# Two-layer decoder, expert layer: hidden columns in four chunks of 896, ScalarE's hand-overs one split earlier

## The reference

```python
def swiglu(h, wg, wu, wd):
    return (jax.nn.silu(h @ wg) * (h @ wu)) @ wd

def moe_swiglu(h, w_router, w_gate, w_up, w_down):
    logits = (h @ w_router).astype(jnp.float32)
    top_v, top_i = lax.top_k(logits, TOP_K)                 # TOP_K = 2
    top_w = jax.nn.softmax(top_v, axis=-1)
    gates = ...                                             # (tokens, 8), two nonzero a row
    for e in range(N_EXPERTS):                              # 8 experts, EXPERT_FF = 3584
        y = y + gates[..., e:e + 1] * swiglu(h, w_gate[e], w_up[e], w_down[e])
    return y
```

## Time and profile before

| | |
|---|---|
| median of 3 runs | 1429.4 us (1425.54 to 1433.12) |
| profiled execution | 1420.63 us, its span 1418.8 us |
| granted TensorE clock, mean | 0.986 |
| PE busy | 1369.0 us, 96% of the span |
| DVE busy | 1097.6 us, 77% |
| ACT busy | 940.6 us, 66% |
| DMA | 439.13 MB in 136643 packets, mean 310 GB/s |
| chain that ended last | PE 73%, DVE 17%, ACT 5%, DMA 3%, issue 3% |

### The profile page before, as it was taken

The page is one execution under the profiler, slowest core; times in us unless marked ns, Lnnn a source line. Parts: engine busy times, 40 slices in busy tenths (PEclk is TensorE's granted clock), DMA queues, the critical chain, the costliest instruction groups (busy, mean ns, idle before and its releaser), DMA issues.

```text
span 1418.8 us, 16608 instructions
## 1 busy us (share of the span) xinstructions
PE 1369.0 (96%) x6550; PEld 1143.2 (81%) x6550; DVE 1097.6 (77%) x871; ACT 940.6 (66%) x767; POOL 49.3 (3%) x51
## 2 busy tenths in 40 slices
PE   8999999999999999999999999999999999999887
PEld 7886788887988788877888878878887878888766
DVE  4786644556465988888898898798898889888796
ACT  3565534335455677777777788687777777777764
POOL 0000000000010000000000000000000000002000
PEclk9999999999999999999999999999999999999998
DMA  9744455555632899999999999999999989999993
GB/s 311 214 159 149 155 205 178 178 179 177 224 119 92 334 373 382 379 387 399 322 407 390 364 400 407 393 366 398 379 374 414 408 324 397 394 368 392 412 360 115
DMA packets 136643, 439.13 MB, mean 310 GB/s; under 512 B 11520, under 2 KB 28912, under 8 KB 120816
## 3 DMA queue, kind: packets, MB, share of 16 engines
q1 hardware_dynamic: 130688, 424.24, 80.0%
q0 software_dynamic: 3392, 12.07, 2.5%
q10 hardware_dynamic: 2480, 1.69, 0.4%
HBM read 432.20 MB, written 5.78 MB: 309 GB/s over the span
## 4 chain that ended last, share of the span: by engine, by line
PE 73%; DVE 17%; ACT 5%; DMA 3%; issue 3%; ACTq 0%; SPq 0%; DVEq 0%
PE ps L2003 18%; PE ps L2005 18%; PE ps L2004 18%; DVE lo L1286 12%; PE ps L2575 7%; PE ps L2495 4%; PE ps L2496 4%; ACT hi L790 2%; DMA raw<-in_od_w_gate_dram 2%; PE ps L2560 1%; DMA wr<-in_od_w_router_dram 1%; ACT work L1098 1%; DVE work L1312 0%; PE ps L2299 0%; DMA x<-in_x_dram 0%
## 5 line engine op out<-in xcount | busy, mean ns | idle before, releaser
L1286 DVE TENSOR_TENSOR lo<-raw,hi 128x2048 fp32r<-128x2048 f32 (+1 forms) x403 | 904.9, 2285 | 102.9 <-ACT hi L790 101.2
L790 ACT ACTIVATE hi<-raw 128x2048 fp32r<-128x2048 f32 (+1 forms) x403 | 766.8, 1914 | 206.4 <-PE ps L2005 157.0
L2003 PE MATMUL ps<-hi,xT_hi 128*128 128x512 f32 (+1 forms) x752 | 294.6, 392 | 7.2 <-DVE lo L1286 4.6
L2005 PE MATMUL ps<-hi,xT_lo 128*128 128x512 f32 (+1 forms) x752 | 290.0, 386 | 0.0
L2004 PE MATMUL ps<-lo,xT_hi 128*128 128x512 f32 (+1 forms) x752 | 289.7, 385 | 0.0
L2495 PE MATMUL ps<-hi,xT_hi 128*128 128x512 f32 x448 | 187.4, 418 | 12.0 <-DVE lo L1286 11.0
L2496 PE MATMUL ps<-lo,xT_hi 128*128 128x512 f32 x448 | 181.4, 405 | 0.0
L2003 PEld LDWEIGHTS ps<-hi,xT_hi 128*128 128x128 f32 x752 | 141.7, 188 | 38.3 <-issue 5.5
L2005 PEld LDWEIGHTS ps<-hi,xT_lo 128*128 128x128 f32 x752 | 141.4, 188 | 28.7
L2004 PEld LDWEIGHTS ps<-lo,xT_hi 128*128 128x128 f32 x752 | 141.6, 188 | 26.4
L2495 PEld LDWEIGHTS ps<-hi,xT_hi 128*128 128x128 f32 x448 | 88.5, 198 | 45.5 <-DVE lo L1286 19.9
(11 more groups left out here) (327 smaller groups left out, 1223.9 us busy)
## 6 DMA issues: line engine op xcount, KB each, us to landing
raw<-in_od_w_gate_dram SPq DMA_DIRECT2D x112, 1024.0 KB, 8.4
raw<-in_od_w_up_dram SPq DMA_DIRECT2D x112, 1024.0 KB, 9.4
raw<-in_od_w_down_dram SPq DMA_DIRECT2D x112, 1024.0 KB, 8.3
raw<-in_od_w_qkv_dram SPq DMA_DIRECT2D x12, 1024.0 KB, 5.2
raw<-in_ev_w_gate_dram SPq DMA_DIRECT2D x11, 1024.0 KB, 5.2
raw<-in_ev_w_up_dram SPq DMA_DIRECT2D x11, 1024.0 KB, 5.1
raw<-in_ev_w_down_dram SPq DMA_DIRECT2D x11, 1024.0 KB, 5.1
raw<-in_ev_w_in_dram SPq DMA_DIRECT2D x4, 1024.0 KB, 11.1
```

Source lines behind the costliest of these rows:

```text
L790: act.activation(unit(hi, n), unit(raw, n), ACT.Copy).then_inc(hi_ready, 1)
L1286: dve.tensor_tensor(unit(lo, n), unit(raw, n), unit(hi, n).bitcast(F32), ALU.subtract)\
L2003: pe.matmul(out, s_hi, m_hi, start=start, stop=False, skip_group_check=True)
L2005: return pe.matmul(out, s_lo, m_hi, start=False, stop=stop, skip_group_check=True)
```

## The change

All four chunks are 896 columns wide. A gate or up unit now holds 2 k-tiles of 896 columns (1792 numbers a partition, DMA packets of 3584 bytes), and TensorE runs 512 and 384 of the columns as two matmuls. The 7 row tiles of a chunk's down matrix come in four units of 2, 2, 1 and 2 tiles. An expert is 48 units. Hand-overs are eight an expert, of 4 and 3 tiles in turn, two for each chunk; the second of the first chunk (s = 1) is new in its place. In small experts ScalarE's `used(...)` ahead of `keep_gate`, `keep_up`, `turned_silu` and `turned_high` is lowered by one, so that two units are split ahead where three were. VectorE's are not lowered. Large experts keep their `used(...)`. At the start of an expert TensorE waits for all gathered columns, not for half of them. The dense branch is changed in the same way.

```diff
 MOST = NE * P + NE - 1
-MOE_CHUNKS = [(0, W)] + [(f, 2 * W) for f in range(W, EFF, 2 * W)]
+MC = EFF // 4
+MJ = MC // P
+MOE_CHUNKS = [(f, MC) for f in range(0, EFF, MC)]
+DOWN_PARTS = [(0, 2), (2, 2), (4, 1), (5, 2)]
...
     def down(c):
         down_at.append(len(order))
-        order.extend(("down", c, q) for q in range(2 * MOE_CHUNKS[c][1] // W))
+        order.extend(("down", c, q) for q in range(len(DOWN_PARTS)))
 
     for c, (_, w) in enumerate(MOE_CHUNKS):
         for kind, starts in (("gate", gate_at), ("up", up_at)):
             starts.append(len(order))
-            order.extend((kind, c, q) for q in range(KD * w // UNIT))
+            order.extend((kind, c, q) for q in range(KD // (UNIT // w)))
...
-        kind, c, _ = moe_order[(n - U_MOE) % PER]
-        w = D if kind == "down" else MOE_CHUNKS[c][1]
+        kind, c, q = moe_order[(n - U_MOE) % PER]
+        if kind == "down":
+            return DOWN_PARTS[q][1], D
+        w = MOE_CHUNKS[c][1]
         return UNIT // w, w
+
+    def pieces_of(w):
+
...
-        NSUB = EFF // W
-        SUBS = [list(range(f // W, (f + w) // W)) for f, w in MOE_CHUNKS]
         NCH = len(MOE_CHUNKS)
+        NSUB = 2 * NCH
+        SUBS = [[2 * c, 2 * c + 1] for c in range(NCH)]
+        SUB_J = [(0, 4), (4, MJ - 4)]
...
-                        src = down_w[SUBS[c][q // 2], :, 2 * (q % 2):2 * (q % 2) + 2, :]
+                        first, count = DOWN_PARTS[q]
+                        src = down_w[c, :, first:first + count, :]
...
@@ ScalarE, small experts
-                        used(UP_AT[0])
+                        used(UP_AT[0] - 1)
                         keep_gate(e, 0)
-                        used(GATE_AT[1])
+                        used(GATE_AT[1] - 1)
                         keep_up(e, 0)
+                        used(GATE_AT[1] + 1)
+                        turned_silu(e, 0)
                         used(GATE_AT[1] + 2)
-                        turned_silu(e, 0)
-                        used(GATE_AT[1] + 3)
                         turned_high(e, 0)
+                        used(UP_AT[1] - 1)
+                        turned_silu(e, 1)
+                        keep_gate(e, 1)
                         used(UP_AT[1])
-                        keep_gate(e, 1)
-                        used(DOWN_AT[0])
+                        turned_high(e, 1)
+                        used(DOWN_AT[0] - 1)
                         keep_up(e, 1)
                         used(GATE_AT[2])
                         if e == NE - 1:
                             act.wait_ge(placeT_done, 1)
                             act.activation(placeT[:], ps[:, 6, 0:SEQ], ACT.Copy).then_inc(placeT_ready, 1)
+                        used(GATE_AT[2] + 1)
+                        turned_silu(e, 2)
                         used(GATE_AT[2] + 2)
-                        turned_silu(e, 1)
-                        used(GATE_AT[2] + 3)
-                        turned_high(e, 1)
+                        turned_high(e, 2)
+                        used(UP_AT[2] - 1)
+                        turned_silu(e, 3)
+                        keep_gate(e, 2)
                         used(UP_AT[2])
-                        turned_silu(e, 2)
-                        keep_gate(e, 2)
-                        used(UP_AT[2] + 1)
-                        turned_high(e, 2)
-                        used(DOWN_AT[1])
+                        turned_high(e, 3)
+                        used(DOWN_AT[1] - 1)
                         keep_up(e, 2)
+                        used(GATE_AT[3] + 1)
+                        turned_silu(e, 4)
                         used(GATE_AT[3] + 2)
-                        turned_silu(e, 3)
-                        used(GATE_AT[3] + 3)
-                        turned_high(e, 3)
+                        turned_high(e, 4)
+                        used(UP_AT[3] - 1)
+                        turned_silu(e, 5)
+                        keep_gate(e, 3)
                         used(UP_AT[3])
-                        turned_silu(e, 4)
-                        keep_gate(e, 3)
-                        used(UP_AT[3] + 1)
-                        turned_high(e, 4)
+                        turned_high(e, 5)
+                        used(DOWN_AT[2] - 1)
+                        keep_up(e, 3)
                         used(DOWN_AT[2])
-                        keep_up(e, 3)
+                        turned_silu(e, 6)
                         used(DOWN_AT[2] + 1)
-                        turned_silu(e, 5)
+                        turned_high(e, 6)
                         used(DOWN_AT[2] + 2)
-                        turned_high(e, 5)
-                        used(DOWN_AT[2] + 3)
-                        turned_silu(e, 6)
+                        turned_silu(e, 7)
                         used(DOWN_AT[3])
                         if e + 1 < NE:
                             gathered_high(e + 1)
-                        turned_high(e, 6)
+                        turned_high(e, 7)
                         continue
...
@@ ScalarE, large experts
                     silu(e, 1)
+                    g_hT_high(e, 1)
                     used(GATE_AT[2])
                     if e == NE - 1:
...
@@ VectorE, small experts
+                        turned_multiply(e, 1)
+                        used(UP_AT[1] + 1)
+                        turned_low(e, 1)
...
-                        turned_multiply(e, 1)
+                        turned_multiply(e, 2)
                         used(GATE_AT[2] + 3)
-                        turned_low(e, 1)
+                        turned_low(e, 2)
                         used(UP_AT[2])
-                        turned_multiply(e, 2)
+                        turned_multiply(e, 3)
                         used(UP_AT[2] + 1)
-                        turned_low(e, 2)
+                        turned_low(e, 3)
                         if e + 1 < NE:
...
@@ TensorE, a gate or up unit
-                    for m in range(w // W):
-                        cols = slice(W * m, W * m + W)
+                    for m, cols in pieces_of(w):
+                        out = ps[:, bank + m, 0:cols.stop - cols.start]
                         if e in SMALL:
-                            ins = both(ps[:, bank + m, :], xg_hi[:, k, :], wh[:, kk, cols], wl[:, kk, cols], k == 0,
+                            ins = both(out, xg_hi[:, k, :], wh[:, kk, cols], wl[:, kk, cols], k == 0,
                                        k == KD - 1)
                             continue
-                        ins = three(ps[:, bank + m, :], xg_hi[:, k, :], xg_lo[:, k, :], wh[:, kk, cols],
+                        ins = three(out, xg_hi[:, k, :], xg_lo[:, k, :], wh[:, kk, cols],
                                     wl[:, kk, cols], k == 0, k == KD - 1)
                 ins.then_inc(units_used, 1)
 
...
@@ TensorE, a down unit
-                        j = 2 * (q % 2) + jj
+                        if jj >= count:
+                            continue
+                        j = first + jj - SUB_J[s % 2][0]
...
@@ TensorE, a hand-over in a small expert
-                f = W * (s - SUBS[c][0])
+                first, count = SUB_J[s % 2]
                 for part in range(2):
-                    for j in range(4):
-                        first = SEQ * part + HALF * j
-                        ins = pe.matmul(ps[:, 7, first:first + HALF], work[:, part, f + j:f + W:4], fold64[:],
+                    for j in range(count):
+                        out = SEQ * part + HALF * j
+                        ins = pe.matmul(ps[:, 7, out:out + HALF], work[:, part, first + j:MC:MJ], fold64[:],
                                         start=True, stop=True)
                 ins.then_inc(g_hT_done, 1)
...
@@ TensorE, order of the work
-                    pe.wait_ge(xg_ready, 2 * e + 1)
-                    gate(e, 0, 0)
                     pe.wait_ge(xg_ready, 2 * e + 2)
-                    gate(e, 0, 1)
-                    up(e, 0, 0, 1)
+                    gate(e, 0, 0, 1, 2, 3)
+                    up(e, 0, 0, 1, 2, 3)
                     gate(e, 1, 0, 1)
                     if e in SMALL:
                         if e == SMALL[0]:
                             pe.wait_ge(order_ready, 1)
                         turn(e, 0, 0)
                         gate(e, 1, 2, 3)
+                        turn(e, 1, 0)
                         up(e, 1, 0, 1, 2, 3)
                         pe.wait_ge(y_copied, e)
-                        down(e, 0, 0, 1)
+                        down(e, 0, 0, 1, 2, 3)
                         if e == NE - 1:
                             transpose_place(e)
                         gate(e, 2, 0, 1)
-                        turn(e, 1, 1)
+                        turn(e, 2, 1)
                         gate(e, 2, 2, 3)
-                        turn(e, 2, 1)
+                        turn(e, 3, 1)
                         if e + 1 < NE:
                             pick_rows(e + 1)
                         up(e, 2, 0, 1, 2, 3)
```

(8 more changed lines are left out.)

156 lines of the change are left out of this document (85 added, 71 removed).

## The result

| | before | after |
|---|---|---|
| median | 1428.4 us (4 runs) | 1464.9 us (1461.77 to 1467.83, 4 runs) |
| profiled execution, its span | 1420.63, 1418.8 us | 1461.77, 1459.6 us |
| mean granted clock | 0.986 | 0.992 |
| large experts 2, 4, 6 | 116.6 us each | 119.0 us each |
| small experts 1, 3, 5, 7 together | 482.2 us | 510.2 us |

The ratio after to before is **1.0261, 95% interval 1.0233 to 1.0289: slower**, 36.5 us at the median. The forecast was 1455, its own range 1443 to 1468. An expert's length here is from VectorE's first split of it to its first of the next, the last one's to TensorE's last matmul.

What follows compares the result with a forecast made beforehand. TensorE was taken to bound large experts, VectorE's splits plus stalls small ones. 4 x 7.0 + 2.6 = +30.6 us gave 1451 or 1460, middle 1455 us; own range 1443 to 1468, 8 in 10 from 1425 to 1475.

Steps and rivals of the forecast that it cites:

- Small experts are paced by VectorE and its stalls: Small experts: VectorE's splits plus stalls set the pace, the DMA stream just behind; +7.0 us each.
- The walk of the pair: Two successive hand-overs in a small expert, timed step by step: VectorE stalls of 2.07, 1.26 and 2.1 us, 5.4 a pair.
- the late u0: First up unit of a pair, split by ScalarE only after the silu; its lateness hides 1.24 us ahead of the second product.
- What would show it: Signs in the new trace: VectorE idle 1.3 and 2.1 us behind products, silu wait longer by a split, GB/s lower.
- VectorE's and ScalarE's prices: Split of 1792 numbers: 1.95 us on VectorE, 1.70 us on ScalarE; `keep_gate` of 896 columns 0.9 us.
- Large experts, the step that was mis-sized: Large experts, bound by TensorE: 48 more matmuls at 0.013 us fixed each, +0.64 us an expert, +2.6 us for four.
- The stream: DMA of expert weights: as many packets and bytes, 412 GB/s, so 0; the skill's fixed cost would give 96 us.
- The sum: Whole kernel: +30.6 us, 1451 from the profiled execution, 1460 from the median 8.8 us above it; middle taken, 1455 us.
- ScalarE late (faster): Rival at the hand-overs: ScalarE's lateness is real, an earlier hand-over saves 1 us off each of 28; 1404 us, chance 0.12.
- The stream swallows the stalls: Rival in small experts: DMA sets the pace, the raw ring absorbs new stalls; only +2.6, 1432 us, chance 0.10.
- The clock falls more: Rival in small experts: TensorE's stalls lower its clock by a further 0.04, 19 us; 1474 us, chance 0.09.
- Smaller units slow the stream: Rival in every expert: DMA rate falls with the ring to 7/8 of 412 GB/s; about +70, 1498 us, chance 0.03.

Runs made afterwards that it cites:

- a_three: Kernel after with ScalarE's used(...) in small experts raised by one again, so three units are split ahead, not two: 1441.8 us, ratio 1.0085.
- f_512: Kernel after, but in large experts the second column piece of gate and up is 512 columns wide, not 384: 1498.9 us (1 run).
- b_dve3: Kernel before with VectorE's product in small experts put one low split later: 1427.1 us, ratio 0.9987.
- b_both: Kernel before with ScalarE's hand-overs one high split later and VectorE's product one low split later in small experts: 1431.1 us, ratio 1.0003.
- b_near: Kernel before with both those orders one split later in small experts and `turned_high` right behind `turned_silu`: 1426.4 us, ratio 0.9979.
- b_two: Kernel before with ScalarE's used(...) in small experts lowered by one, as in the change: 1460.1 us, ratio 1.0216.

## Why the prediction was right, step by step

- **Small experts are paced by VectorE and its stalls.** The mechanism is right: in the four of them VectorE has 5.7 us more work and 22.3 us more idle time (94.6 for 72.3), which is the 28.0. By the profile of a_three, 19 us of the 28 are the order's and 9 the chunks'; by the medians the chunks' part here is less, since a_three is 12 us above before and 9.5 of these lie in large experts. That +7.0 us each was forecast and +7.0 came (28.0 / 4) is in part luck. In expert 3, with as much low clock in both traces, +10.4 came: 6.3 by the hand-overs' stalls (20.0 for 13.8; +6.2 was forecast), 2.4 by waits of 0.2 to 1.0 us ahead of other splits (4.0 for 1.6), which the walk put at none, and 1.6 by work, forecast at 1.1. In experts 1, 5 and 7 the walk's shortfall met a clock that fell less often, for which the prediction had no term.
- **The walk of the pair.** Stall behind the first product 1.26, measured 1.17; ahead of the second 0 and 0; behind the second 2.1 and 2.04. What the late u0 swallows ahead of the second product, 1.24 in the walk, is 1.31 in a_three where the clock stays up. Two terms were off: the stall ahead of the first product is 1.34 to 1.57, not 2.07, so a pair has 4.7 and not 5.4; and the last pair has 6.0 and not 4.5, as VectorE is through with the down units 2.86 us before the product is there. 3 x 5.4 + 4.5 = 20.7 was forecast, 20.0 came (4.55, 4.78, 4.68 and 6.00); the errors cancelled. The walk's test against the old trace, 3.7 us a pair for 3.7, was right in its sum only: it had 2.07 and 1.24 ahead of the two products where the rows have 1.22 and 2.12, and the second of these stands beside a fall of the clock (at 868.05). The period of a pair is 30.4 to 31.0 us for a forecast of 30.1.
- **What would show it.** ScalarE's wait at the silu grew from 2.4 us to 3.9 for the four-tile turns (61.8 / 16) and fell to 2.0 for the three-tile ones (32.5 / 16); "by a split" held for the first kind only. The stream fell to 361 GB/s in small experts as said.
- **VectorE's and ScalarE's prices.** 1.95 us for VectorE's split back to back: four took 7.56, 1.89 each; ScalarE's 1.70 us: 1.699. `keep_gate` 0.9: 0.917.
- **Large experts, the step that was mis-sized.** +0.64 us each was forecast, +2.4 measured, 9.6 for 2.6 on the sum. The fixed part of 0.013 us for 48 more matmuls stood; what the rows of before did not show is that a piece below 512 columns makes its neighbours dearer (f_512 takes it away): gate and up cost 2.1 us more. The bound "longer than 118 us" in the prediction was broken, by this.
- **The stream.** 0 was right for the packets: one of 3584 bytes takes 0.140 us at the median, between 0.084 for 2048 and 0.159 for 4096, and the stream ran at 375 GB/s in a large expert. The gate DMAs landed sooner than in the earlier trace rows:

```profile
raw<-in_od_w_gate_dram SPq DMA_DIRECT2D x128, 896.0 KB, 7.2
```

  By the 2.0 us fixed for each DMA in the Trainium skill, "DMA: Bandwidth & Descriptors", section "Anatomy of one DMA — SWDGE (gpsimd) path" (the prediction quotes it beside the section Bandwidth; it is a fit of DMAs that GpSimd issues, and here SyncE does), the estimate was 96 us more; a_three, with all 48 DMAs an expert, is 12 us above before, and the large experts hold 9.5 of these with TensorE busy throughout. The fit does not carry over to these DMAs, which are queued one behind another.
- **The sum.** 1451 on the profile was 1461.8: 7.0 us by the large experts and 3.2 by the later start. The instructions ahead of the experts are the same; that start lies between 456.2 and 460.3 us in the kernels of this study, and its cause was not looked for. Between 1451 and 1460 the prediction took the middle; the profiled execution of after is 3 us below its median, that of before 8 us, so part of the 8.8 us was to be added. The prediction had no row for them; the later runs of before fit the clock, 0.986 in the profiled one and a median of 0.981 to 0.982 in the others.
- **The rivals.** ScalarE late (faster): refuted; b_dve3, b_both and b_near took up to 42 of the 54.9 us at the product away and gained 0.2% at the median. The stream swallows the stalls: refuted by the period of 30.4 us, by a_three and by b_two. The clock falls more: refuted, it rose (0.992 for 0.986 in the profiles), and so hid part of the loss. Smaller units slow the stream: refuted by a_three.

## What to carry to other kernels

In a queue that runs in order, an instruction that waits for another engine holds up everything behind it: before it is moved, count for how long the waiting instruction stands there and who needs what is now queued behind it, one place too early and one too late both cost 2% here. A wait that is named in a profile is worth what is late behind it, not its length; it has to be shown by moving it, and each time it was moved here nearly all of it came back elsewhere; add up an engine's waits over all its lines before calling one of them won. Before two traces are compared, compare the clock of the same stretches in both. Cut the moving side of matmuls into full 512-column pieces: a narrower one cost more than its own fixed part.
